# A longer ring for gathered V rows, and six of the last twelve V rows summed on VectorE, in a one-core hybrid attention + PEER layer

## What is computed

```python
def peer_ffn(x, w_query, sub_keys, u, v):      # x normalised, 256 x 1024
    ...
        q = (xc @ w_query).reshape(PEER_CHUNK, PEER_HEADS, 2, PEER_D_HALF)
        sc = jnp.einsum('chpd,hpnd->chpn', q, sub_keys).astype(jnp.float32)
        ...                                     # top 16 of 128 keys, twice; top 16 of the pairs
        g = jax.nn.softmax(best, axis=-1)
        u_sel = u[experts]
        v_sel = v[experts]
        h = jax.nn.gelu(jnp.einsum('cd,chkd->chk', xc, u_sel), approximate=False)
        act = (h.astype(jnp.float32) * g).astype(v_sel.dtype)
        return jnp.einsum('chk,chkd->cd', act, v_sel)
```

## Time and profile before

| | before |
|---|---|
| median of 3 runs | 842.15 us (841.99 to 843.25) |
| the profiled execution's own time | 842.34 us |
| its span in the profile | 840.4 us |
| PE / VectorE / ScalarE / GpSimd busy | 82% / 63% / 29% / 60% |
| gathers' share of the 16 DMA engines' span (queue q0) | 80.7% |
| HBM read | 296.36 MB, 354 GB/s over the span |

### The profile page before, as it was taken

The page is one execution under the profiler, slowest core; times in us unless marked ns, Lnnn a source line. Parts: engine busy times, 40 slices in busy tenths (PEclk is TensorE's granted clock), DMA queues, the critical chain, the costliest instruction groups (busy, mean ns, idle before and its releaser), DMA issues.

```text
span 840.4 us, 7396 instructions
## 1 busy us (share of the span) xinstructions
PE 687.5 (82%) x2133; PEld 370.0 (44%) x2133; DVE 533.5 (63%) x1422; ACT 240.9 (29%) x600; POOL 503.3 (60%) x535
## 2 busy tenths in 40 slices
PE   5999999599898989796667777767777777788888
PEld 4877788555444545453223333322233233333333
DVE  5579554995556675766676766576667576654540
ACT  7568752322312121212121212121213031212110
POOL 7000100777676777677776777777677777677751
PEclk9999999889999999999999999999999999888889
DMA  8844311899999999999999999999999999999994
GB/s 327 305 151 151 101 51 51 320 405 394 394 407 408 410 408 410 408 410 408 409 410 409 409 410 409 411 410 410 408 409 409 409 409 410 409 408 409 409 347 140
DMA packets 91977, 297.91 MB, mean 354 GB/s; under 512 B 8721, under 2 KB 17058, under 8 KB 91938
## 3 DMA queue, kind: packets, MB, share of 16 engines
q0 software_dynamic: 73728, 268.47, 80.7%
q1 hardware_dynamic: 18210, 28.98, 10.0%
HBM read 296.36 MB, written 1.05 MB: 354 GB/s over the span
## 4 chain that ended last, share of the span: by engine, by line
DMA 45%; PE 25%; POOL 13%; DVE 8%; issue 6%; ACT 2%; SPq 0%; POOLq 0%; DVEq 0%; ACTq 0%
DMA v_rows<-in_peer_v_dram,expert 25%; DMA u_rows<-in_peer_u_dram,expert 19%; PE bank L1282 13%; POOL u_rows L393 9%; POOL v_rows L401 4%; PE xg L1046 3%; PE bank L1245 2%; PE bank L1046 2%; DVE u_rows L981 2%; PE bank L1104 1%; DVE w_lo L724 1%; DVE t_nmax L754 1%; DVE logits L751 1%; DMA x_sb<-in_x_dram 1%; PE bank L1031 0%
## 5 line engine op out<-in xcount | busy, mean ns | idle before, releaser
L1282 PE MATMUL bank<-v_rows,diag 128*128 128x512 f32 x1024 | 497.6, 638 | 131.8 <-DMA v_rows<-in_peer_v_dram,expert 127.0
L981 DVE CUSTOM_DVE_ANT_0 u_rows<-u_rows,xg 128x1024 f32<-128x1024 f32 x256 | 310.5, 1220 | 205.4 <-DMA u_rows<-in_peer_u_dram,expert 197.6
L1282 PEld LDWEIGHTS bank<-v_rows,diag 128*128 128x128 f32 x1024 | 202.2, 204 | 398.8 <-issue 384.3
L393 POOL DMA_INDIRECT u_rows<-in_peer_u_dram,expert x256 | 243.7, 952 | 137.7 <-issue 68.3
L401 POOL DMA_INDIRECT v_rows<-in_peer_v_dram,expert x256 | 239.8, 937 | 115.1 <-PE bank L1282 58.5
L656 ACT ACTIVATE h_gelu<-h_dot 128x4 f32<-128x4 f32 x64 | 12.9, 202 | 347.8 <-DVE h_dot L981 347.8
L662 ACT ACTIVATE diag<-ident,act_w 128x128 f32<-128x128 f32 x256 | 84.3, 389 | 10.8 <-DVE act_w L995 6.0
L1245 PE MATMUL bank<-featT,w_raw 128*128 128x128 f32 (+1 forms) x384 | 62.7, 315 | 4.6 <-ACT qT L626 4.6
L1245 PEld LDWEIGHTS bank<-featT,w_raw 128*128 128x128 f32 x384 | 56.2, 196 | 19.5 <-issue 11.8
L313 POOL TENSOR_TENSOR normed<-qk_raw,t_qk_rs 128x512 f32<-128x512 f32 x4 | 4.1, 1043 | 66.5 <-DVE t_qk_rs L820 66.5
L626 ACT ACTIVATE qT<-bank 128x128 f32<-128x128 f32 (+1 forms) x24 | 7.5, 313 | 114.9 <-PE bank L1245 114.9
(11 more groups left out here) (167 smaller groups left out, 513.1 us busy)
## 6 DMA issues: line engine op xcount, KB each, us to landing
w_raw<-in_w_in_dram SPq DMA_DIRECT2D x12, 1024.0 KB, 7.2
w_raw<-in_peer_w_query_dram SPq DMA_DIRECT2D x8, 1024.0 KB, 11.6
w_raw<-in_w_out_dram SPq DMA_DIRECT2D x4, 1024.0 KB, 5.1
u_rows<-in_peer_u_dram,expert POOLq DMA_INDIRECT x256, 16.0
v_rows<-in_peer_v_dram,expert POOLq DMA_INDIRECT x256, 16.0
x_sb<-in_x_dram SPq DMA_DIRECT2D x2, 512.0 KB, 3.8
out_dram<-y_rows SPq DMA_DIRECT2D x2, 512.0 KB, 4.7
g_row<-in_norm_g_dram SPq DMA_DIRECT2D x1, 512.0 KB, 13.0
```

The lines of the kernel that those rows point to most:

```text
L393: pool.indirect_dma_start(u_rows[:, n % U_RING, :], None, peer_u[0], bass.IndirectOffsetOnAxis(ap=expert[:, u, s:s + 1], axis=0))\
L981: dve.tensor_tensor_reduce(out=u_rows[:, n % U_RING, :], in0=u_rows[:, n % U_RING, :], in1=xg[:, :, :].rearrange("p c n -> p (c n)"), scal ...
L1282: ins = mm(ps[y_bank(h, c)][:, :], diag[:, n % DIAG_RING, :], v_rows[:, n % V_RING, c * COLS:(c + 1) * COLS], start=False, stop=True, skip ...
```

## The change

The ring for V rows gets 11 places instead of 8. It now begins where the dead features lie (behind `diag`), with the U ring behind it; `w_lo` moves ahead of the other attention buffers so that its place lies under the V ring. The end of the arena stays where it was.

Of the last twelve V rows, six (`ADDED_ROWS`) are skipped by TensorE and by ScalarE's diagonals. VectorE, after its last `weights`, waits for each to land and sums weight x row into a new tile `added` (one multiply, then five multiply-adds). The final copies out of PSUM become two additions of `added`, both on VectorE, 512 columns each, and SP stores each 512 columns as soon as they are ready.

```diff
-V_RING = 8
+V_RING = 11
+ADDED_ROWS = (245, 247, 249, 251, 253, 254)
...
-    u_rows = whole.put("u_rows", [P, U_RING, D])
-    v_rows = whole.put("v_rows", [P, V_RING, D])
-    arena_at = whole.at
...
     over = Region(xn_at)
     diag = over.put("diag", [P, DIAG_RING, P])
-    assert over.at <= stream_at
+    v_rows = over.put("v_rows", [P, V_RING, D])
+    u_rows_at = over.at
+    u_rows = over.put("u_rows", [P, U_RING, D])
+    arena_at = over.at
...
     y_rows = over.put("y_rows", [P, HALVES, D])
+    added = over.put("added", [P, D])
...
+        def multiplied(n):
+
+            return n - sum(r < n for r in ADDED_ROWS)
...
-            for h in range(HALVES):
-                sp.wait_ge(y_ready[h], 2)
-                sp.dma_start(out[0, h * P:(h + 1) * P, :], y_rows[:, h, :]).then_inc(stored, 16)
-            sp.wait_ge(stored, 16 * HALVES)
+            sp.wait_ge(y_ready[0], 2)
+            sp.dma_start(out[0, 0:P, :], y_rows[:, 0, :]).then_inc(stored, 16)
+            for c in range(2):
+                sp.wait_ge(y_ready[1], c + 1)
+                sp.dma_start(out[0, P:SEQ, c * COLS:(c + 1) * COLS], y_rows[:, 1, c * COLS:(c + 1) * COLS]).then_inc(stored, 16)
+            sp.wait_ge(stored, 16 * 3)
...
-                need(pool, v_used, n - V_RING + 1)
+                if n - V_RING in ADDED_ROWS:
+                    pool.wait_ge(v_added, ADDED_ROWS.index(n - V_RING) + 1)
+                else:
+                    need(pool, v_used, multiplied(n - V_RING + 1))
...
-                        diagonal(n)
+                        if n not in ADDED_ROWS:
+                            diagonal(n)
...
-            act.wait_ge(v_used, GATHERS)
-            act.activation(y_rows[:, 1, COLS:D], ps[y_bank(1, 1)][:, :], ACT.Copy).then_inc(y_ready[1], 1)
...
-            dve.wait_ge(v_used, GATHERS)
-            dve.tensor_copy(y_rows[:, 1, 0:COLS], ps[y_bank(1, 0)][:, :]).then_inc(y_ready[1], 1)
+            for k, n in enumerate(ADDED_ROWS):
+                u, s = divmod(n, TOPK)
+                row, weight = v_rows[:, n % V_RING, :], act_w[:, u, s:s + 1]
+                dve.wait_ge(act_ready, n // GROUP + 1)
+                dve.wait_ge(v_landed[n % V_RING], 16 * (n // V_RING + 1))
+                if k == 0:
+                    dve.tensor_scalar(added[:, :], row, weight, None, ALU.mult).then_inc(v_added, 1)
+                else:
+                    dve.wait_ge(v_added, k)
+                    dve.scalar_tensor_tensor(added[:, :], row, weight, added[:, :], ALU.mult, ALU.add).then_inc(v_added, 1)
+            dve.wait_ge(v_added, len(ADDED_ROWS))
+            dve.wait_ge(v_used, multiplied(GATHERS))
+            for c in range(2):
+                cols = slice(c * COLS, (c + 1) * COLS)
+                dve.tensor_tensor(y_rows[:, 1, cols], ps[y_bank(1, c)][:, :], added[:, cols], ALU.add).then_inc(y_ready[1], 1)
...
             for n in range(GATHERS):
...
-                pe.wait_ge(diag_ready, n + 1)
+                if n in ADDED_ROWS:
+                    continue
+                m = multiplied(n)
+                pe.wait_ge(diag_ready, m + 1)
```

More of the change, by code:

```diff
@@ L139, in layer @@
     over = Region(stream_at)
+    w_lo = over.put("w_lo", [P, W_PARTS, 4, COLS], F32R)
+    assert over.at <= u_rows_at
     qkT = over.put("qkT", [P, 4, 4, SEQ])
@@ L146, in layer @@
     probsT = over.put("probsT", [P, 2, 3 * P])
-    assert over.at >= arena_at - 4 * V_RING * D
-    w_lo = over.put("w_lo", [P, W_PARTS, 4, COLS], F32R)
     assert over.at <= arena_at
@@ L256, in layer @@
         v_used = sem("v_used")
+        v_added = sem("v_added")
         y_ready = [sem(f"y_ready{h}") for h in range(HALVES)]
@@ L660, in diagonal @@
                 u, s = divmod(n, TOPK)
-                need(act, v_used, n - DIAG_RING + 1)
-                act.activation(diag[:, n % DIAG_RING, :], ident[:, :], ACT.Copy, scale=act_w[:, u, s:s + 1])\
+                m = multiplied(n)
+                need(act, v_used, m - DIAG_RING + 1)
+                act.activation(diag[:, m % DIAG_RING, :], ident[:, :], ACT.Copy, scale=act_w[:, u, s:s + 1])\
                    .then_inc(diag_ready, 1)
@@ L1278, in _ @@
                 h = u // PEER_HEADS
-                pe.wait_ge(diag_ready, n + 1)
+                if n in ADDED_ROWS:
+                    continue
+                m = multiplied(n)
+                pe.wait_ge(diag_ready, m + 1)
                 pe.wait_ge(v_landed[n % V_RING], 16 * (n // V_RING + 1))
                 for c in range(2):
-                    ins = mm(ps[y_bank(h, c)][:, :], diag[:, n % DIAG_RING, :],
+                    ins = mm(ps[y_bank(h, c)][:, :], diag[:, m % DIAG_RING, :],
                              v_rows[:, n % V_RING, c * COLS:(c + 1) * COLS],
```

## The result

| | before | changed |
|---|---|---|
| median | 842.15 us | 837.94 us (5 runs, 837.2 to 838.96) |
| profiled execution, span | 842.34, 840.4 | 837.2, 835.4 |
| GpSimd / VectorE / PE busy | 60% / 63% / 82% | 60% / 65% / 82% |

The ratio is 0.9945 (95% interval 0.9935 to 0.9956): 0.55% faster, where 0.6% was forecast. In the profiles 5.0 us went, where 5.2 were forecast. The profiled execution of the changed kernel is the fastest of its five runs, so the medians show 4.2 us.

A forecast was written before the change was run, and what follows sets the result against it. Transfers bound the steady part and PE the tail, whose landings a lagging DMA engine sets. PE's end -5.2, additions +0.7 and store -0.7 sum to -5.2 us: 837.0 us on the median, range 834.0 to 839.5.

The forecast's parts named there:

- The bound of the tail: Last V rows: one lagging DMA engine sets landings 1.28 us apart until 829.6, whatever the issue time.
- The ring, 0 us: V ring of 11 places: last V row issued 5.6 us earlier, gain 0, bounds 0 and 5.6 us.
- Six rows off PE, -5.2 us: PE's tail: 10.4 us of work taken off, landings take half back, PE ends at 831.4 instead of 836.6.
- VectorE hidden: VectorE's six rows in the tail: summed by 829.6, at the worst 831.1, before PE is done at 831.4.
- The way out: After PE's end: two additions in a row cost 0.7 us more, the half-size last store 0.7 less (bounds 0 and 1.3).
- The clock: PE in the tail: gaps of 0.8 and 2.1 us might lower its clock from 2.4 to 1.2 GHz.
- B: Rival, PE's clock falls in the tail: last V row alone, 838.7 us, 8%; all from 246 on, 841.1 us, 3%.

The follow-up runs named there:

- the ring of 8: Changed kernel with 8 V ring places in use instead of 11, other edits kept: 837.28 us, ratio 0.9941 to the kernel before; 0.9974 in the disturbed hour.
- the version by columns: Changed kernel with the last V rows shared by columns between PE and VectorE, row 255 VectorE's alone: 836.20 us, ratio 0.9927 to the kernel before.

## Why the prediction was right, point by point

- **The bound of the tail.** "That one sets the landings, and it does not care when GpSimd issues": shown by the ring alone (5 us earlier issue, same landing) and by the stretch with a share of 0.05. From PE's start of V row 244 to the last landing it is 13.9 us before, 13.8 in the changed kernel, 13.8 with the ring alone, 13.9 with the ring of 8 and 13.8 with ScalarE's extra instructions, while the last issue moves from 817.4 to 823.1 (the version by columns took 14.1).
- **The ring, 0 us**: the ratio is 0.9998. But this holds only where the rate is even; the prediction named no condition, and in the uneven hour 0 was wrong (ratio 0.9950).
- **Six rows off PE, -5.2 us**: PE's end moved from 836.6 to 831.45, 5.1 us. The gaps are 0.6 and 1.85 instead of 0.8 and 2.1, since a row alone takes 1.95 us; 1.74 is the pace of rows that follow one another.
- **VectorE hidden**: multiply 0.75 (taken 0.87), multiply-add 1.28 to 1.35 (taken 1.22), sums done at 829.6 as worked out, PE 1.85 us later. The prediction's "at the worst 831.1" was added up wrongly: at its own bound of 2.4 us an operation the last two rows would have been summed at 827.1 + 4.8 = 831.9, behind PE's 831.4. The cover was thinner than it said; the measured 1.28 to 1.35 us left it whole.
- **The way out**: additions 1.29 for 1.38; the second store saved 0.5 for 0.7. From PE's end to the end of the span it is 3.95 us against 3.8 before, where the forecast had the same: 0.1 lost.
- **The clock**: PEclk 1.00 (the level of 2.4 GHz) in all stretches from 810 to 830. Gaps of 0.6 and 1.85 us did not bring it down, so B did not happen.
- **The number**: 837.0 forecast, 837.94 measured: 4.2 us gained by the medians, not 5.2. By the profiles the sum is off by only 0.2 us, the two items above. The step that is off by most is that one execution stood for all: the profiled execution before lies 0.2 above its median, that of the changed kernel 0.7 below. The last landing lies between 829.0 and 830.1 over the even profiles, and V row 244, ahead of the tail, shifts with it (815.15 to 816.22). Two versions whose landings are bound in the same way, the ring of 8 and ScalarE's extra instructions, have medians of 837.28 and 837.24 us. So most of the missing microsecond can be which executions were met; no run shows more.

## What to carry to other kernels

Before taking work off the engine that is busy at the end, work out when the last data land: issue plus landing of the last few transfers, and the distance between landings against the distance between issues. If landings keep their own distance, the transfer is the next bound, and only the work up to it can be won (here 5.1 of 10.4 us, and three rows did nearly what six did). After that bound, what counts is how much must follow the last landing in series; sharing the last tiles by columns took 2.0 us off that in the profile, 1.7 by the medians.

## What was not expected of the hardware

One DMA engine's worth of transfer was left over while the rest had ended: they ran dry between 821 and 824 us, and a share of 0.06 at 25 GB/s went on alone until 829, with the last landing at 829.3. That landing did not depend on the depth of the queue (8 or 11 places) nor on 480 more ScalarE instructions; which engine it is and why it lags stays open. The other surprise is the size of what a disturbed hour does to a kernel that reads 296 MB: 914 to 923 us instead of 842, and a ring that is worth 0.5% there and nothing on an even chip.
